# RMS-norm sums over the model dimension in a single-core transformer kernel: part of the addition moved from TensorE to VectorE, and the sums moved to other places among the first projection tiles

## The reference, cut to what matters

```python
def rmsnorm(t, g):                      # the first block ends with rmsnorm(x, g_final)
    y = tf * lax.rsqrt(jnp.mean(tf * tf, axis=-1, keepdims=True) + NORM_EPS)
    return (y * g.astype(jnp.float32)).astype(t.dtype)
...
def second_block(x, ...):
    for i in range(DEPTH_2):            # two layers: i = 0 (SSD mixer), i = 1 (LRU mixer)
        h = rmsnorm_2(x, norm_mix_pre[i])
        m = ssd_mixer(h, ...) if i % 2 == 0 else rglru_mixer(h, ...)
        x = x + rmsnorm_2(m, norm_mix_post[i])
        h = rmsnorm_2(x, norm_ffn_pre[i])
        f = conv_ffn(h, ...)            # h @ w_up, convolution, gelu gate, @ w_down
        x = x + rmsnorm_2(f, norm_ffn_post[i])
    return x
```

## Time and profile before

| | us |
|---|---|
| median of 3 runs (lowest, highest) | 2596.39 (2594.34, 2596.93) |
| the profiled execution, its own time | 2596.07 |
| its span from first to last instruction | 2594.3 |
| PE busy | 2216.8 |
| DVE busy | 901.9 |
| ACT busy | 363.4 |
| stretch of the second block (1483 to 2594), about | 1111 |

### The profile page before, as it was taken

How to read it: one execution, slowest core, us unless ns; L and a number is a source line. 1 busy time by engine, 2 the same in 40 slices (tenths; PEclk the granted TensorE clock), 3 DMA queues, 4 the chain that set the end, 5 groups by cost and what they waited for, 6 DMA issues and landing times.

```text
span 2594.3 us, 28428 instructions
## 1 busy us (share of the span) xinstructions
PE 2216.8 (85%) x11512; PEld 1560.9 (60%) x11512; DVE 901.9 (35%) x2005; ACT 363.4 (14%) x725; POOL 1.2 (0%) x16
## 2 busy tenths in 40 slices
PE   6999999976667666666666699999999998999999
PEld 4877888842222222222222278788888877788888
DVE  6795895130010000000010165626131325433232
ACT  2231111120000000000000112502010114101011
POOL 0000000000000000000000000000000000000000
PEclk9999999988888788878888889999999999999999
DMA  7525663449999999999999943044444431444420
GB/s 273 182 91 202 227 227 106 193 190 428 428 428 428 428 429 428 428 428 428 429 428 429 411 166 130 33 150 149 155 158 140 155 116 51 161 170 157 160 99 17
DMA packets 147471, 638.05 MB, mean 246 GB/s; under 512 B 10277, under 2 KB 52782, under 8 KB 119486
## 3 DMA queue, kind: packets, MB, share of 16 engines
q1 hardware_dynamic: 146446, 634.79, 62.7%
q10 hardware_dynamic: 944, 2.13, 0.2%
HBM read 635.86 MB, written 1.05 MB: 246 GB/s over the span
## 4 chain that ended last, share of the span: by engine, by line
PE 70%; DMA 23%; DVE 5%; ACT 1%; issue 1%; SPq 0%; ACTq 0%; DVEq 0%
DMA arena<-in_w_down_dram 23%; PE PS L1668 16%; PE PS L1110 12%; PE PS L1681 7%; PE PS L1023 7%; PE PS L1453 4%; PE PS L1497 2%; PE PS L1444 2%; PE PS L1480 2%; PE PS L1340 2%; PE PS L1467 2%; DVE arena L1785 2%; PE PS L1632 2%; PE PS L1034 1%; PE PS L1741 1%; PE PS L1363 1%
## 5 line engine op out<-in xcount | busy, mean ns | idle before, releaser
L1453 PE MATMUL PS<-arena,hT 128*32 128x512 f32 x2048 | 306.6, 742 | 164.5 <-DMA arena<-in_w_up_dram 138.8
L1668 PE MATMUL PS<-arena 128*128 128x256 f32 x1920 | 416.7, 379 | 0.0
L1668 PEld LDWEIGHTS PS<-arena 128*128 128x128 f32 x1920 | 364.8, 190 | 49.6
L1453 PEld LDWEIGHTS PS<-arena,hT 128*32 128x32 f32 x2048 | 66.8, 126 | 385.3 <-DMA arena<-in_w_up_dram 212.5
L1467 PE MATMUL PS<-arena,hT 128*32 128x512 f32 x1024 | 171.3, 804 | 101.0 <-DMA arena<-in_w_down_dram 93.7
L1110 PE MATMUL PS<-hT,arena 128*128 128x256 f32 (+1 forms) x1136 | 253.7, 383 | 1.5 <-ACT hT L699 1.5
L1785 DVE SCALAR_TENSOR_TENSOR arena<-arena 128x512 f32<-128x512 f32 (+2 forms) x514 | 246.5, 547 | 0.9
L1110 PEld LDWEIGHTS PS<-hT,arena 128*128 128x128 f32 (+1 forms) x1136 | 213.4, 190 | 39.4 <-issue 9.7
L1782 DVE TENSOR_SCALAR arena<-arena,cols 128x256 f32<-128x256 f32 x162 | 66.4, 410 | 427.1 <-ACT arena L940 360.7
L1023 PE MATMUL PS<-arena 128*128 128x256 f32 (+1 forms) x864 | 194.9, 386 | 6.1 <-ACT arena L879 5.4
L1681 PE MATMUL PS<-arena 128*128 128x256 f32 x896 | 195.9, 379 | 0.0
(11 more groups left out here) (274 smaller groups left out, 1802.7 us busy)
## 6 DMA issues: line engine op xcount, KB each, us to landing
arena<-in_w_gate_dram SPq DMA_DIRECT2D x64, 2048.0 KB, 40.9
arena<-in_w_up_dram SPq DMA_DIRECT2D x64, 2048.0 KB, 40.7
arena<-in_w_down_dram SPq DMA_DIRECT2D x64, 2048.0 KB, 37.6
arena<-in_ffn_w_up_dram SPq DMA_DIRECT2D x32, 2048.0 KB, 8.9
arena<-in_w_in_dram SPq DMA_DIRECT2D x36, 1024.0 KB, 8.0
arena<-in_ffn_w_down_dram SPq DMA_DIRECT2D x16, 2048.0 KB, 8.0
arena<-in_w_ada_dram SPq DMA_DIRECT2D x12, 2048.0 KB, 11.9
arena<-in_ssd_w_in_dram SPq DMA_DIRECT2D x10, 2048.0 KB, 11.8
```

Of the source, the lines that this page charges most:

```text
L1453: mm = pe.matmul(PS[32 * f:32 * f + 32, 1 + half, :], xe[:, 32 * (2 * pi + k):32 * (2 * pi + k) + 32], w[:, k, 512 * f:512 * f + 512], sta ...
L1668: mm = pe.matmul(PS[:, n, T * half:T * half + T], slot(TAIL_SLOT[j], 8, 512)[:, k, P * n:P * n + P], hs[:, k, :], start=(k == 0), stop=(k ...
```

## The change

The squares are still made by ScalarE in four pieces. VectorE now adds piece 1 and piece 2 to piece 0, element by element, in place (`add_squares`), so that blocks 0 and 1 hold the sums of blocks 0, 2, 4 and 1, 3, 5. For the post norms it also folds block 1 into block 0 (`fold`). It raises a new semaphore, `sq_added`. TensorE sums what is left: blocks 0, 1, 6, 7 for `final` and the pre norms (4 products in place of 8), blocks 0, 6, 7 for the post norms (3 in place of 8), and 6 in place of 16 one-column products for `ffn_post1`. In `raw_tiles` the sums stand behind block 5 instead of 3 (for `mix_pre0`: the final one behind block 2, its own behind block 3). In `last_rows` nothing stands between the banks any more; the three products come after the fourth bank. Several semaphores on which VectorE waits for itself are merged into one, `dve_chain`.

```diff
@@ last_rows
                     close_bank(b, b0).then_inc(s["row_ps"], 1)
-                    if b == 0:
-                        pe.wait_ge(s["std_ready"], NORM[name][0])
-                    elif sums:
-                        bank_sum(name, b - 1)
                 if sums:
-                    bank_sum(name, 3).then_inc(s["ss_ps"], 1)
...
+                    pe.wait_ge(s["std_ready"], NORM[name][0])
+                    pe.wait_ge(s["sq_added"], ADDED[name])
+                    dst = PS[:, norm_bank(name), 0:T]
+                    pe.matmul(dst, ones, sq[:, 0, :], start=True, stop=False, skip_group_check=True)
+                    pe.wait_ge(s["sq_ready"], PIECE0[name] + 4)
+                    pe.matmul(dst, ones, sq[:, 6, :], start=False, stop=False, skip_group_check=True)
+                    pe.matmul(dst, ones, sq[:, 7, :], start=False, stop=True, skip_group_check=True
+                              ).then_inc(s["ss_ps"], 1)
@@ raw_tiles
+            def added_sum(name, src):
+
+                pe.wait_ge(s["sq_added"], ADDED[name])
+                for k in (0, 1, 6, 7):
+                    if k == 6:
+                        pe.wait_ge(s["sq_ready"], PIECE0[name] + 4)
+                    mm = pe.matmul(PS[:, norm_bank(name), 0:T], ones, src[:, k, :], start=(k == 0), stop=(k == 7),
+                                   skip_group_check=True)
+                mm.then_inc(s["ss_ps"], 1)
...
-                    if k == 3:
-                        for other, src in more:
-                            square_sum(other, src)
-                        square_sum(name, oaT if more else sq)
+                    for norm, src, at in sums:
+                        if k == at:
+                            added_sum(norm, src)
...
+                      [("final", sq, 2), ("mix_pre0", oaT, 3)]).then_inc(used, ST.incs["ssd_x"][0])
...
+                raw_tiles(norm, slot(TAIL_SLOT[0], 8, 512), [(norm, sq, 5)]).then_inc(used, 1)
@@ the last norm, on TensorE
-            for c in range(TC):
-                for k in range(KD):
-                    if k % 2 == 0:
-                        pe.wait_ge(s["sq_ready"], PIECE0["ffn_post1"] + k // 2 + 1)
+            pe.wait_ge(s["sq_added"], ADDED["ffn_post1"])
+            for k in (0, 6, 7):
+                if k == 6:
+                    pe.wait_ge(s["sq_ready"], PIECE0["ffn_post1"] + 4)
+                for c in range(TC):
                     mm = pe.matmul(PS[:, 4 + c, 0:1], sq[:, k, P * c:P * c + P], ones[:, 0:1], start=(k == 0),
@@ VectorE
+            def add_squares(name, src, p, fold=False):
+
+                dve.wait_ge(s["sq_ready"], PIECE0[name] + p + 1)
+                ins = tt(src[:, 0:2, :], src[:, 0:2, :], src[:, 2 * p:2 * p + 2, :], ALU.add)
+                if fold and p == 2:
+                    link("mix_tmp", ins)
+                    ins = tt(src[:, 0, :], src[:, 0, :], src[:, 1, :], ALU.add)
+                if p == 2:
+                    ins.then_inc(s["sq_added"], 1)
+                else:
+                    link("mix_tmp", ins)
...
                 ts(hT[:, k, :], xT[:, k, :], gg[:, k:k + 1], None, ALU.mult).then_inc(s["xg_ready"], 1)
+                if k == 5:
+                    add_squares("final", sq, 1)
+            add_squares("final", sq, 2)
+            for p in (1, 2):
+                add_squares("mix_pre0", oaT, p)
             rms("final")
...
                         ts(hT[:, k, :], src, bias(k), gain(k), ALU.add, ALU.mult).then_inc(s["m_ev"], 1)
+                    if k in (3, 5):
+                        add_squares(name, sq, k // 2, True)
...
                         ts(hT[:, k, :], xT[:, k, :], pre_gain(k), None, ALU.mult).then_inc(s["xg_ready"], 1)
+                    if p >= 2:
+                        add_squares(pre, sq, p - 1)
                 rms(pre)
```

More of the change, by code:

```diff
@@ L246 @@
 POST = ("mix_post0", "ffn_post0", "mix_post1", "ffn_post1")
+ADDED = {n: i + 1 for i, n in enumerate(("final", "mix_pre0", "mix_post0", "ffn_pre0", "ffn_post0", "mix_pre1",
+                                         "mix_post1", "ffn_pre1", "ffn_post1"))}
 SEMS = ["x_loaded", "pos_loaded", "bias_in", "const_loaded", "early_loaded", "small_loaded", "router_in",
         "rows_t", "cols_ready", "x_t", "x_ready", "cond_ready", "ada_row", "ada_col", "mod_ready",
-        "pos_chain", "rope_ready", "pos_done", "bias_hot", "bias_dve", "bias_fold", "near_ready", "far_t", "far_bt", "far_ps", "far_hot", "far_out", "far_ready", "sq_ready", "ss_ps",
+        "dve_chain", "rope_ready", "pos_done", "bias_hot", "bias_dve", "bias_fold", "near_ready", "far_t", "far_bt", "far_ps", "far_hot", "far_out", "far_ready", "sq_ready", "sq_added", "ss_ps",
         "std_ready", "rstd_ready", "h_ready", "h1_act", "h1_dve", "pj_ps", "pj_ev", "rot_ps", "rope_tmp", "rope_out",
-        "s_ps", "s_read", "max_chain", "nmx_ready", "p_exp", "rden_ready", "p_norm", "pt_ps", "pt_ev",
+        "s_ps", "s_read", "nmx_ready", "p_exp", "rden_ready", "p_norm", "pt_ps", "pt_ev",
         "o_ps", "o_ev", "o_read", "g_ready", "oa_gated", "mix_tmp", "mix_ready", "x1_ps", "x_new", "h2_part",
-        "wr_zero", "lgt_ps", "lgt_ev", "lg_ps", "rt_chain", "nrmx_ready", "lg_exp", "aff_ready", "aft_ps",
+        "wr_zero", "lgt_ps", "lgt_ev", "lg_ps", "nrmx_ready", "lg_exp", "aff_ready", "aft_ps",
         "h2t_ps", "h2t_ready", "diag_ready", "selb_ps", "sel_ready", "gi_in", "gi_ps", "gi_ready",
@@ L1488, in _, with raw_tiles @@
                     expert(3 * i + 1 + u, 12 + 12 * u, i, False)
-            def raw_tiles(name, w, more=()):
+            def added_sum(name, src):
[6 more added lines that the diff above has]
+                mm.then_inc(s["ss_ps"], 1)
+            def raw_tiles(name, w, sums):
                 r = PRE.index(name)
@@ L1507, in _ @@
             arrived("ssd_x", 0)
-            raw_tiles("mix_pre0", slot(ST.slots["ssd_x"][0], 8, 512), [("final", sq)]
-                      ).then_inc(used, ST.incs["ssd_x"][0])
+            raw_tiles("mix_pre0", slot(ST.slots["ssd_x"][0], 8, 512),
+                      [("final", sq, 2), ("mix_pre0", oaT, 3)]).then_inc(used, ST.incs["ssd_x"][0])
             w = slot(ST.slots["ssd_dt"][0], 8, 32)
@@ L1709, in _ @@
             arrived("lru_in", 0)
-            raw_tiles("mix_pre1", slot(ST.slots["lru_in"][0], 8, 512)).then_inc(used, ST.incs["lru_in"][0])
+            raw_tiles("mix_pre1", slot(ST.slots["lru_in"][0], 8, 512), [("mix_pre1", sq, 5)]).then_inc(used, ST.incs["lru_in"][0])
             for j in range(1, 5):
@@ L1795, in rms @@
                 dve.wait_ge(s["rstd_ready"], i + 1)
-            pc = "pos_chain"
+            pc = "dve_chain"
             dve.wait_ge(s["const_loaded"], 16)
@@ L2049, in _ @@
                 tt(hT[:, 2 * p:2 * p + 2, :], xT[:, 2 * p:2 * p + 2, :], both, ALU.mult).then_inc(s["h2_part"], 1)
-            rc = "rt_chain"
+            rc = "dve_chain"
             dve.wait_ge(s["lg_ps"], 1)
@@ L2176, in log1p_series @@
                 link(sem, ts(w, w, 2.0, None, ALU.mult))
-            dc = "dt_chain"
+            dc = "dve_chain"
             dve.wait_ge(used, ST.pos["ssd_dt"][0] + 1)
@@ L2352, in _ @@
             post_dve("mix_post0", gain_of("norm_mix_post_2"), "ffn_pre0", gain_of("norm_ffn_pre_2"))
-            lc = "lam_chain"
+            lc = "dve_chain"
             lam = cols[:, COL["lru_lambda_2"]:COL["lru_lambda_2"] + NL]
```

15 lines of the change are left out of this document (6 added, 9 removed).

## The result

The changed kernel takes 2576.86 us (median of 4 runs, 2575.57 to 2576.99) against 2596.36 before (4 runs, 2594.34 to 2596.93): ratio 0.9925, interval 0.9912 to 0.9938, 19.5 us less. The forecast was 2581, 2577 to 2587. But the gain was 4.2 us larger than forecast, and the median lies just outside the range. Two later sets of four runs of the same kernel, each timed beside the kernel before, gave 2578.99 and 2578.88 against 2596.06 and 2594.99: 17.1 and 16.1 us less. Over the three sets the 12 runs of the changed kernel have a mean of 2578.1 us and the 38 of the kernel before one of 2595.8: 17.7 us apart, by their spread good to about 1 us. So some 1.8 of the 4.2 us were the luck of the first set, and some 2.4 are in the mean as well.

What follows compares the result with a forecast made beforehand. The prediction took TensorE, busy nearly throughout the chain from 1483 us on, to be the bound. Its terms summed to 15.25 us off the profiled 2596.07, plus 0.3 for the median: forecast 2581, range 2577 to 2587.

Steps and rivals of the forecast that it cites:

- The nine terms: Gains forecast norm by norm for the nine norms, from sum products leaving TensorE's path: 15.25 us together.
- `mix_pre0` 3.46: Sums of `final` and `mix_pre0`: 16 products become 8, VectorE's additions hidden, gain 3.46 us.
- `mix_post0` 1.83: Sums between the banks of `mix_post0` go, worth 1.73 us, and the root comes 0.10 sooner: 1.83 us.
- `mix_post1` 1.3: Sums between the banks of `mix_post1` go, but TensorE waits nearly 1 us for the fold: gain 1.3 us.
- the pre norms 5.18: `ffn_pre0`, `mix_pre1`, `ffn_pre1`: 4 products fewer each, with additions and norm factor hidden: 5.18 us.
- `ffn_post0` 1.73: In `ffn_post0` four products go and nothing else changes: 1.73 us.
- The thin cover: At the three pre norms, eight raw products (3.45 us) hide the norm factor's chain of 3.08, with 0.37 us over.
- The last term: `ffn_post1`: ten narrow products go, then the root waits for ScalarE's table load, output products following as before: 1.75 us.
- the term of the slow restarts: Restarts at half clock behind idle times: nothing in the sum; as a rival 10%, up or down, 2577 to 2587.
- The late factor: Rival, 8%: norm factor late at three pre norms, TensorE waits before its first `hs` tile; gain 10.1 us, 2586.
- A loss of the full clock: Rival, 2%: bank stretches and raw tiles lose the full clock; slower than before, 2607 with 12 slow products per restart.
- No gain: Rival, 3%: the sums had been free because VectorE set the raw tiles' pace; time stays at 2596.

Runs made afterwards that it cites:

- e12: Kernel before with the change for `final` and the four pre norms alone, post norms and `ffn_post1` summed as before: 2588.50 us, ratio 0.9975.
- e1: Kernel before with products of constants filling TensorE's five idle times, results unchanged: 2585.93 us.
- e4: Changed kernel with VectorE adding the fourth piece and folding, so `final` and the pre norms need one product per sum: 2571.93 us.
- e3: Changed kernel with the sums of `ffn_pre0`, `mix_pre1` and `ffn_pre1` behind block 6 instead of 5: 2583.17 us.
- e5: Changed kernel with one product per sum for `final` and the pre norms, and TensorE's five idle times filled with products of constants: 2563.02 us.
- e13: Changed kernel with idle times filled and the sums of `ffn_pre0`, `mix_pre1` and `ffn_pre1` behind block 3 instead of 5: 2571.38 us.
- e15: Kernel before with the five idle times filled, profiled a second time: 1101.5 us from the first raw tile of `mix_pre0` to the end.
- e6: Changed kernel with two products of constants added in front of `mix_pre0`'s own sum: 2578.90 us.
- e7: Changed kernel with four products of constants added in front of `mix_pre0`'s own sum: 2577.95 us.

## What the prediction had right, and the step that failed

**The nine terms.** `mix_pre0` 3.46 (measured from its first raw tile to the first narrow product: 21.59 to 18.13, 3.46), `mix_post0` 1.83 (root against last tile: 1.84), `mix_post1` 1.3 (1.32, with the wait of 0.94 that I had put at nearly 1), the pre norms 5.18 and `ffn_post0` 1.73: together 13.5, and 13.5 in the ledger, in three traces of each kernel. e12 splits it into the 8.6 of `final` and the pre norms and the 4.9 of the three post norms. The additions take 0.69 us at 128x512, and the only one that TensorE waits for is the fold in `mix_post1`. The thin cover held, with 0.24 us instead of 0.37.

**The last term** was 1.75 and measured 2.0 (tails of 10.2, 10.0, 10.1 against three of 8.1). The root did move by 1.75 (4.08 us behind the last close before, 2.33 now). But I had taken VectorE's output products as unchanged. Before, they followed transposes that took 3.05 us, now 1.95, and they take 2.73 instead of 3.09. This is the clock once more, in the transposes of the kernel before and of the changed one, and in e1:

```profile
2588.60:2591.00 2.40, 2.40 (x13) 2.01 (x10) 2.16 (x4) 0.00 (x0) 0.00 (x0) 0.51 0.27 102
2569.07:2571.02 1.95, 1.95 (x18) 1.71 (x17) 1.28 (x3) 0.59 (x2) 0.00 (x0) 1.00 0.00 0
2576.18:2579.83 3.65, 3.65 (x17) 3.25 (x17) 2.42 (x4) 0.27 (x1) 0.00 (x0) 0.50 0.20 74
```

So this term has no fixed size: with the tails of e1 and e12 against 8.1 it would be 3.3 and 3.9 us.

**The step that failed** is the term of the slow restarts. The prediction says that the change leaves the idle times as long as they were, "but moves them", and puts the effect at nothing in the sum; as a rival it gets 10% for both directions, with a size of 4 us downwards (2577). The idle times of TensorE ahead of the raw tiles are indeed as long, 4.41 us in both kernels (4.50 in `mix_pre1` of the changed one); ahead of the tile in the SSD mixer they move between 4.2 and 5.4 us with the execution. But the losses behind the five restarts came to 2.9 us less in the first pair and 2.2 less in the mean of three traces, and the narrow products to 0.5 less. The 13.5 of the ledger, 2.0 of the tail, 2.2 and 0.5 make 18.2 us, which is the mean difference of the stretches. I had two rows of single losses, 1.77 and 3.00, and counted five such restarts. That is some 12 us of the stretch, worked out from two rows, and a term of this size should have had a wider range of its own.

**Luck.** The gain of the first set was 1.8 us above the mean gain of all sets. With the mean time, 2578.1, the forecast would have been 2.9 us off, and the result inside its range. That the losses came out lower and not higher was nothing that I had foreseen.

**What stays open.** Why the changed kernel loses less at its restarts, and whether it does so as a property of its own. Six sums of losses, three and three, fall apart like this (12.7 to 13.5 against 9.9 to 11.4) in one case of ten by chance alone. And close relatives of the changed kernel lost 11.8 (e4), 12.5 (e12) and 13.0 us (e3). The runs without a trace say more: 17.7 us between the means, good to about 1, against 15.5 for the ledger's 13.5 and the tail's 2.0. So a surplus of some 2 us is probably in the kernel and not only in the draw. It need not be the restarts: the tail of the kernel before can be 1 to 2 us longer than in its three traces, as e1 and e12 show. I made no experiment that sets the losses at will, except filling the idle time. That removed them at 27 of 30 filled restarts in six traces; one in e5, one in e13 and one in e15 were slow all the same.

**The rivals.** The late factor did not occur behind block 5 and appeared at once behind block 6. A loss of the full clock in the bank stretches and at the dense raw tiles did not occur; where it fell with TensorE busy was at the narrow and the one-column products, which the prediction did not name. No gain: excluded by 16.1 to 19.5 us in three sets.

## What to carry to other kernels

When a chain is one engine deep, count instructions by the row's price and ask of each dependent chain what covers it: that gave 13.5 us of 13.5. Keep apart from this sum what the clock does behind each idle time, list those places with their losses, and give them a range of their own; a second trace of the kernel before would have shown a single loss move by 1.65 us (the SSD mixer, 3.31 and 1.66). And where TensorE must wait some 4 us for another engine, products that nobody needs, ended just before the wait does, were worth 1.4 to 3 us each time here; at 3 of 30 filled restarts the loss came all the same.

## What was not expected of the hardware

A restart behind 4.4 us of idle time costs between 1.6 and 3.3 us for the same products: half of the 2.8 to 6.2 us for which the granted clock then stood at 0.50, and 0.2 us beside. With 8 products of constants in the idle time, 0.96 us of idle left, it costs 0.2.

The granted clock also fell while TensorE was busy. Sixteen products with 32 columns took 4.1 us where it stayed at 1.00 (e6, e7) and 5.4 us where it fell 1.8 us behind their start. In the kernel before it fell 4.6 to 4.8 us behind the last close, in the transposes that follow 16 one-column products: 3.7 us for these and 3.1 for the transposes. Where it fell 3.3 or 2.6 us behind the close, these took 4.3 and 3.7 (e1) or 4.9 and 3.7 (e12). With 6 one-column products the transposes took 1.95 us in every trace: they were over 3.9 us behind the close, and the clock fell 6.1 us behind it or later.
